# Reordering the last layer's mixing of a three-layer network into one interleaved programme

## The reference

```python
h  = rms(x)*norm1_w*(1+sc1)+sh1          # and hc from the context, the same way
p  = h @ w_in                            # 1024 -> u,v | q | k,v | qh,zf,zb,vh | g
ya = gelu(u) * (w_s @ rms(gelu(v)) + b_s)              # 4 heads of 64
q, k = rope(rms(q)*q_norm_w), rope(rms(k)*k_norm_w)    # 8 query heads, 2 key heads
yb = softmax(q @ [k,kc].T / 8) @ [v,vc]                # 256 queries, 512 keys
# gated recurrence in both directions, 4 heads of 64; log_f, key from zf (forward), zb (backward)
s_new  = exp(b_last)*s + (key*exp(b_last-b)).T @ vh     # state from the context first
o      = (qh*exp(b)) @ s + (scores within a chunk, each with its own decay) @ vh
yc = rms(o_forward + o_backward)*hgrn_norm_w * silu(g)
x  = x + g1 * (concat(ya, yb, yc) @ w_out)
h2 = rms(x)*norm2_w*(1+sc2)+sh2          # then router and 32 experts
```

## Time and profile before

| | |
|---|---|
| median of 3 runs | 1739.26 us (1736.14 to 1740.77) |
| profiled execution | 1736.32 us |
| its span | 1734.5 us |
| PE, DVE, ACT, POOL busy | 93%, 27%, 21%, 2% of the span |
| DMA, mean over the span | 309 GB/s |

### The profile page before, as it was taken

How to read it: one execution, slowest core, us unless ns; L and a number is a source line. 1 busy time by engine, 2 the same in 40 slices (tenths; PEclk the granted TensorE clock), 3 DMA queues, 4 the chain that set the end, 5 groups by cost and what they waited for, 6 DMA issues and landing times.

```text
span 1734.5 us, 20614 instructions
## 1 busy us (share of the span) xinstructions
PE 1617.4 (93%) x8418; PEld 901.9 (52%) x8418; DVE 473.0 (27%) x1118; ACT 368.1 (21%) x770; POOL 34.0 (2%) x44
## 2 busy tenths in 40 slices
PE   5999879999989988999998996897799999999998
PEld 3664654444465647444444782345644444444444
DVE  2044331212123234312122123463311212121212
ACT  2142221111122234211112311442211111111111
POOL 0000000000000000000000001040000000000000
PEclk9999989999999998999999996897799999999999
DMA  9996649999999567699998100004269999999995
GB/s 320 386 386 246 245 166 427 428 429 428 414 335 331 194 243 321 281 427 428 428 429 329 49 1 0 1 1 194 97 286 425 429 429 429 429 429 428 428 427 238
DMA packets 94672, 535.17 MB, mean 309 GB/s; under 512 B 7935, under 2 KB 11737, under 8 KB 69922
## 3 DMA queue, kind: packets, MB, share of 16 engines
q1 hardware_dynamic: 94258, 534.41, 75.8%
q10 hardware_dynamic: 368, 0.12, 0.0%
HBM read 533.44 MB, written 1.06 MB: 308 GB/s over the span
## 4 chain that ended last, share of the span: by engine, by line
PE 85%; DMA 5%; DVE 4%; SPq 2%; ACT 2%; issue 1%; DVEq 0%; POOL 0%; ACTq 0%
PE pair L901 24%; PE bank L890 7%; PE pair L908 6%; PE bank L630 6%; PE bank L908 6%; DMA ring<-in_w_dram 4%; PE bank L637 3%; PE bank L591 3%; PE bank L951 3%; PE pair L951 3%; PE bank L724 2%; SPq L403 1%; DMA ring<-in_a_w_qkv_dram 1%; PE bank L1047 1%; PE pair L1112 1%
## 5 line engine op out<-in xcount | busy, mean ns | idle before, releaser
L901 PE MATMUL pair<-ring,arena 128*64 128x512 f32 x2048 | 447.3, 594 | 3.5 <-DVE arena L1837 2.9
L901 PEld LDWEIGHTS pair<-ring,arena 128*64 128x64 f32 x2048 | 144.7, 137 | 288.1 <-issue 288.1
L890 PE MATMUL bank<-arena 128*128 128x128 f32 x1120 | 139.5, 279 | 9.4 <-DVE arena L1825 9.4
L1850 DVE TENSOR_TENSOR arena<-sq,pair 128x512 f32<-128x512 f32 x32 | 34.0, 1061 | 408.2 <-PE pair L901 408.2
L890 PEld LDWEIGHTS bank<-arena 128*128 128x128 f32 x1120 | 133.6, 196 | 9.9 <-issue 9.9
L630 PE MATMUL bank<-hh,ring 128*128 128x256 f32 x512 | 120.6, 394 | 6.9 <-ACT hh L1206 3.5
L908 PE MATMUL pair<-ring,arena 128*64 128x512 f32 x512 | 116.9, 598 | 0.0
L908 PE MATMUL bank<-ring,arena 128*64 128x512 f32 x512 | 115.3, 592 | 0.0
L630 PEld LDWEIGHTS bank<-hh,ring 128*128 128x128 f32 x512 | 99.4, 197 | 28.0 <-issue 11.6
L1376 ACT ACTIVATE sq<-pair 128x512 f32<-128x512 f32 x32 | 19.1, 597 | 370.3 <-PE pair L901 370.3
L1858 DVE COPY arena<-bank 128x512 f32<-128x512 f32 x32 | 22.1, 692 | 202.7 <-PE bank L908 202.7
(11 more groups left out here) (375 smaller groups left out, 1623.3 us busy)
## 6 DMA issues: line engine op xcount, KB each, us to landing
ring<-in_w_dram SPq DMA_DIRECT2D x96, 2048.0 KB, 15.6
ring<-in_moe_w_gate_dram SPq DMA_DIRECT2D x32, 2048.0 KB, 11.6
ring<-in_moe_w_up_dram SPq DMA_DIRECT2D x32, 2048.0 KB, 15.9
ring<-in_moe_w_down_dram SPq DMA_DIRECT2D x32, 2048.0 KB, 13.9
ring<-in_ada_w_dram SPq DMA_DIRECT2D x24, 2048.0 KB, 17.4
ring<-in_w_mod_dram SPq DMA_DIRECT2D x12, 2048.0 KB, 12.2
ring<-in_a_w_qkv_dram SPq DMA_DIRECT2D x6, 2048.0 KB, 19.2
ring<-in_b_w_qkv_dram SPq DMA_DIRECT2D x6, 2048.0 KB, 11.7
```

What stands on the lines that cost most here:

```text
L890: last = mm(b[part][:, cols(k % 4)], h_tok[:, t, cols(k)], pick[:, t, :], start=(t == 0), stop=(t == TT - 1))
L901: last = mm(b[2 + m][half(a), :], x_sel[:, k, half(a)], R8[moe_slot(l, a, m)][:, k, :], start=(k == 0), stop=(k == KT - 1))
L1850: tt(hid.rearrange("p (f q) -> p q f", f=FT), by_row(gate_act), by_row(b[3]), ALU.mult).then_inc(M["hid_ready"], 1)
```

## The change

The work of the last layer's mixing is the same; its order and some of its shapes are new.

- The gates' part of the projection is split: the context's 256 columns in four parts (`decay_part`), the first at the end of the second layer's experts and three before the new norm is ready, then the tokens' 256 columns. Then vh, g, qh, k; q, vb, vm and u come later, between steps of the recurrence.
- The recurrence runs both directions in one loop of 16 steps (`steps`, `products`, `decayed`), its state from `update_bank` b[0] to b[3]; each sum over features is two matmuls of half the columns into two neighbouring groups of 32 partitions. State terms accumulate in b[6], opened by a matmul with zeros. `norm_sums`, the spreads, rotations and doublings of q and k stand between steps.
- The heads are done in pairs, 8 units of two heads and 128 queries: one maximum over 2 x 512, negated by the instruction itself, two exponentials, two divisions, eight transposes, two copies; scores and values of the two heads alternate between the halves of the array. The chunk scores, ya and the norm of the recurrence's output stand between units.
- The output projection is in two halves of the 1024 inputs: the first half (`out_first`, two output tiles at a time in b[6]) between the last units, the second after them; both are added to `xT`.
- SP loads the first output chunk after POOL's last addition, the second after the last step, and the first experts' chunks wait for their own slots. `state` now lies in the slot of the second output chunk.

The diff, cut to its core:

```diff
-        IN_ORDER = (3, 4, 0, 1, 2)
+        IN_ORDER = (3, 4, 2, 1, 0)
...
+        add_out(2, 1, 32 + 16)
...
-                            sp.wait_ge(out_ps, 3)
+                            sp.wait_ge(update_ps, 4)
...
+            after_experts(1, moe_at[1], 5)
+            sp.wait_ge(arg_ready, 2 * SUB)
+            load(out_at[2][0])
+            sp.wait_ge(out_ps, 1)
+            load(out_at[2][1])
...
+            def decay_part(idx, at):
+                if idx >= 4:
+                    pe.wait_ge(in_ready, idx - 3)
+                w = chunk_in(in_at)
+                for k in range(KT):
+                    if idx == 4:
+                        pe.wait_ge(h_ready, turn(h_ready))
+                    last = mm(b[idx % 4][:, 0:S], w[:, k, cols(idx % 4)], hh[:, k, at:at + S], start=(k == 0), stop=(k == KT - 1))
+                last.then_inc(in_proj, 1)
...
+                if l == 1:
+                    pe.wait_ge(h_ready, turn(h_ready, KT))
+                    decay_part(0, S)
...
+                def query_in(j):
+                    if j == 0:
+                        pe.wait_ge(act_step, 7)
+                    else:
+                        pe.wait_ge(in_ready, EVAC["k"] + j - 1)
+                    part(17 + j, (x1, x0)[j % 2][:, 0:S], 1, lambda w, k: (w[:, k, cols(j)], hh[:, k, 0:S])).then_inc(in_proj, 1)
...
+                def mix_value_in(t):
+                    pe.wait_ge(norm_ready, 42 if t == 0 else 45)
...
+                def steps(i):
+                    for d in range(2):
+                        q = 2 * i + d
+                        pe.wait_ge(prod_ready, q + 1)
+                        for hp in range(2):
+                            at = 64 * d + 32 * hp
+                            last = mm(seen_part(b[7][at:at + 32, 0:S], q), heads_to(key_of(q)[1]), prod_half(q, hp),
+                                      start=(i == 0), stop=(i == SUB - 1))
+                        last.then_inc(sc_ps, 1)
+                    for d in range(2):
+                        if i >= 1:
+                            pe.wait_ge(state_ready, 2 * i + d)
+                        j = sub_chunk(d, i)
+                        own = slice(j * SUB, (j + 1) * SUB)
+                        for hp in range(2):
+                            for m in range(2):
+                                last = mm(b[6][half(m), hp * S + own.start:hp * S + own.stop], state[half(m), d, hp, i, :],
+                                          qq[half(m), d, hp, own], start=False, stop=False)
+                    if i == SUB - 1:
+                        last.then_inc(out_ps, 1)
...
+                    for m in range(2):
+                        last = mm(score2_pair(u)[:, m, :], q2[half(m), p_, cols(qt)], kd[half(m), p_ // 2, :],
+                                  start=True, stop=True)
...
+                    pe.wait_ge(prob_ready, 16 + u + 1)
+                    if u >= 1:
+                        pe.wait_ge(probT_ready, 16 + u)
+                    for m in range(2):
+                        for kt in range(4):
+                            last = nc.tensor.transpose(b[m][:, cols(kt)], p2[:, u % 2, m, cols(kt)], ident)
...
+                def values(p_):
+                    pe.wait_ge(probT_ready, 16 + 2 * p_ + 2)
+                    if p_ >= 1:
+                        pe.wait_ge(o_ready, 16 + p_ + 1)
+                    for kt in range(4):
+                        for m in range(2):
+                            last = mm(b[7][half(m), 0:S], vb[:, kt, half(p_ // 2)], pT2[:, m, kt, :],
+                                      start=(kt == 0), stop=(kt == 3))
+                    last.then_inc(pv_ps, 1)
...
+                def out_first(n):
+                    if n == 0:
+                        pe.wait_ge(ymix_ready, 2)
+                        pe.wait_ge(o_ready, 19)
+                    else:
+                        pe.wait_ge(x_half, 16 + 2 * n)
+                    w = R4[slot_of_chunk(out_at[2][0])]
+                    chunk_in(out_at[2][0])
+                    for c in (2 * n, 2 * n + 1):
+                        for k in range(4):
+                            last = mm(b[6][:, c % 2 * S:(c % 2 + 1) * S], w[:, k, cols(c)], ymix[:, k, :],
+                                      start=(k == 0), stop=(k == 3))
+                    last.then_inc(out_proj, 2)
...
+                steps(0)
+                query_in(1)
+                steps(1)
+                steps(2)
+                query_in(2)
+                steps(3)
+                steps(4)
+                query_in(3)
+                steps(5)
+                steps(6)
+                value_in(0)
+                steps(7)
...
+                steps(11)
+                rotate_queries(0)
+                steps(12)
+                rotate_queries(1)
+                rotate_keys()
+                mix_value_in(1)
+                steps(13)
...
+                scores(5)
+                out_first(0)
+                transposes(4)
+                scores(6)
+                out_first(1)
+                transposes(5)
+                values(2)
+                scores(7)
+                out_first(2)
+                transposes(6)
+                transposes(7)
+                out_first(3)
+                values(3)
+                for c in range(KT):
...
+                query(0)
+                decayed(0)
+                decayed(1)
+                query(1)
+                decayed(2)
+                decayed(3)
...
+                def products(i):
+                    for d in range(2):
+                        q = 2 * i + d
+                        dve.wait_ge(prod_exp, q + 1)
+                        pr = prod_of(q)
+                        tt(pr, pr, qh.rearrange("p b (j t) -> p (b j) t", t=SUB)[:, :, seen_by(*key_of(q))],
+                           ALU.mult).then_inc(prod_ready, 1)
+                        if i < NSUB - 1:
+                            advance(d, i)
...
                 def maxima(u):
+                    dve.wait_ge(scores_ps, 16 + u + 1)
+                    nc.vector.tensor_reduce(stat[:, u % 4, 0:2], score2_pair(u)[:, :, :], AX.X, ALU.max,
+                                            negate=True).then_inc(max_ready, 1)
...
+                maxima(5)
+                half_out(0)
+                weights(4)
+                maxima(6)
+                half_out(1)
+                weights(5)
+                maxima(7)
+                half_out(2)
+                weights(6)
+                weights(7)
+                half_out(3)
...
```

More of the change, by code:

```diff
@@ new lines, in own_values @@
+                def own_values(hp):
+                    pe.wait_ge(dmT_ready, 2 * hp + 2)
+                    for t in range(TT):
+                        for d in range(2):
+                            for m in range(2):
+                                last = mm(b[6][half(m), hp * S + t * P:hp * S + (t + 1) * P], vh[:, t, half(2 * hp + m)],
+                                          dmT[:, d, 2 * t + m, :], start=False, stop=(hp == 1 and t == TT - 1 and d == 1))
+                    last.then_inc(out_ps, 1)
@@ L1069, in hybrid @@
[L1069 to L1075 removed]
+                for t in range(4):
+                    first_part(8 + t, 4, lambda w, k: (hh[:, k, cols(t)], w[:, k, 0:256]))
+                for j in range(2):
+                    first_part(12 + j, 4, lambda w, k: (w[:, k, cols(2 + j)], hh[:, k, 0:S]))
@@ new lines, in hybrid @@
+                steps(14)
+                double_keys(1)
+                mix_gate_in(0)
+                steps(15)
+                mix_gate_in(1)
+                scores(0)
+                pe.wait_ge(act_step, 8)
+                pe.wait_ge(in_ready, EVAC["u0"])
+                for t in range(TT):
+                    last = nc.tensor.transpose(x0[:, cols(t)], sc_rows[:, cols(t)], ident)
+                last.then_inc(sc_ps, 1)
+                turn_scores(0)
+                turn_scores(1)
@@ new lines, in hybrid @@
+                scores(1)
+                mix()
+                own_values(0)
+                transposes(0)
+                turn_scores(2)
+                turn_scores(3)
+                transposes(1)
+                own_values(1)
+                scores(2)
+                values(0)
+                out_sums()
+                scores(3)
+                transposes(2)
+                out_spread()
+                scores(4)
+                transposes(3)
+                values(1)
+                scores(5)
@@ new lines, in hybrid @@
+                nc.vector.reciprocal(rstd[0:64, :], rt[0:64, :]).then_inc(rs_ready, 1)
+                products(9)
+                products(10)
+                rescale(0)
+                rescale(1)
+                products(11)
+                rescale(2)
+                products(12)
+                rope(0)
+                rope(1)
+                products(13)
+                rope(2)
+                products(14)
+                products(15)
+                maxima(0)
```

(1 more changed line is left out.)

761 lines of the change are left out of this document (398 added, 363 removed).

## The result

The changed kernel takes 1689.47 us (median of four executions, 1686.49 to 1694.90), the kernel before beside it 1739.15. The ratio is 0.972 with a 95% interval of 0.970 to 0.974: 2.8% faster, inside the range, 6.5 us above the forecast. In the first set of experiments it took 1688.06, a ratio of 0.971 (0.969 to 0.973).

The account below looks back on a forecast made before the run. The bound was taken as a dependency chain beside a waiting PE in the last layer's mixing. Stages summed to 243.5 us against 303.7, 60 gained, net 55 after 5 to 6 for the clock: forecast 1683 us, range 1662 to 1705.

Parts of the forecast that it names:

- A: Entry and gates of the last layer's mixing: 29.5 us after the change against 39.3 before, 10 us gained.
- F: Second half of the output projection: 2.16 us a tile, eight times 17.3, and 0.7 at the end, 18 us.
- B: Projections vh, g, qh and k: 34.5 us, with the decays beside them just covered.
- C: From the keys to the first state: 10.5 us, the recurrence starting near 1006 us.
- D: The recurrence with everything between its steps: 77 us, of which PE's work is 67, ending near 1083 us.
- rival 1: Narrow pairs don't run side by side: recurrence 8 us longer, heads 7 longer, 1698 us in all; chance 0.14.
- E: The heads, with the first half of the output projection moved in: 74 us at full clock, to 1157 us.
- 2: Rival: the clock stays at half through the heads, 29 us on the chain less 5 counted, 1707 us; chance 0.09.
- 3: Rival: the recurrence pays the whole round trip, 77 us becomes 156, total time 1762 us; chance 0.03.
- 4: Rival: expert weights are late, PE waits for DMA at the first expert, +10 us, 1693 us; chance 0.02.

## Why the prediction was right, point by point

*A.* 31.1 us against 29.5. The norm's sums were taken at 0.12 us a record; they take 3.45 for sixteen, 0.216 each, the 0.43 for two that the prediction's own F took from the earlier trace rows. The cover by the context parts is as forecast: no idle time, and the experiment that undoes the entry shows 8.5 us.

*B and C.* 34.9 and 11.0 against 34.5 and 10.5. The decays were just covered, with no wait in the stage.

*D.* 74.7 against 77, TensorE busy for 67.4 where 67 was summed. That 67 was met is in part luck: the steps take 18.2 us instead of 23 (sums over features 8.5 for 11, states 9.7 for 12) and what stands between them 49.2 instead of 44, 2.8 of it the half clock at 1020.91, which the prediction held at 1.00. The waits are 7.4 us instead of 10, and they stand where the prediction put them: at the first step, at steps 2, 4, 6 and 8 and at the rotation, and none at 1, 3 and 5. The narrow products run side by side, more so than assumed: four groups at once instead of two, which is rival 1 refuted. How much the work between the steps saves was not priced by itself; undone it costs 10.5 us, in waits and clock together.

*E.* 81.2 against 74 and 5 to 6 for the clock. With the clock held the stage is 73.1: the forecast at full clock stands to 1 us, though its parts less well. There the first output part comes after 39.5 us where 42 was summed, the fourth after 67.1 (66), and the last stretch is 6.0 us instead of 8. The term mis-sized is the clock, 8 us instead of 5 to 6. The milestones as it stands: first transposes 13.3 us after the start (13), first output part 44.4 (42), rounds of 8.6 to 13.2 where 8.05 was taken, since the one with the values is longer. That the output part and its addition lie on the chain was right, and the experiment with the division first shows it. Not seen was the other place of the same kind: the norm's root behind two exponentials, 5.3 us of wait.

*F.* 18.0 against 18, 2.16 us a tile.

*Behind the mixing.* Forecast at no change; norm and router took 1.9 us more. The router's sixteen pairs now run at half rate throughout, where the kernel before had the first five steps from pair to pair at 0.22 to 0.25 us.

Together: 52.8 gained in the mixing instead of 55, then 1.9 and 1.5 lost beside it. (The prediction's 1736.3 - 55 with 2.9 added is 1684.2; it wrote 1683.) Of the 52.8 us, the three parts that were undone one by one stand for 8.5 (entry), 10.5 (work between the steps) and 10.5 (output between the heads) by their stages. The narrow products, both directions in one loop and the pairs of heads were not undone, and their shares rest on the sum and the windows alone. Of the rivals, 2 (half clock all through the heads) was true of 7 or 8 of its 29 us, 3 fell with the first profile (the longest wait of the recurrence is 1.48 us), and for 4 no wait for a DMA stands before the first expert.

## What to carry to other kernels

Where two in-order engines feed each other, look for an instruction that waits at the head of a queue while the one behind it, on which the other engine waits, has its inputs: one such change of order took 9.4 us here without removing any work; a second one beside it took 4 us more from the rest of the stage (55.6 to 51.8), which the time doesn't separate from noise. Price a chained stage twice, at the full and at the half clock, and ask which waits make it fall; filling them with harmless matmuls shows the price at once. Judge an interleaving against the same work in a row at the same clock: here the row showed no more idle time, but TensorE ran at half rate where it would have waited. And before two profiles of a stage are compared, compare a part of it that the edit does not touch.

## What the runs showed that was not expected

- The sums over features of both directions, eight records into four 32-column groups, take 0.55 us from start to start at 240 columns, about what four records take (0.56 at 256).
- The same instructions of the recurrence took 73.1, 74.7, 76.4 or 78.1 us in eleven profiles, 1.6 to 1.7 us apart, at clocks of 0.98, 0.95, 0.93 and 0.91 where these were read. The start of the heads took 13.8 to 14.2 us or 17.6 in the same way.
- Work that only keeps TensorE busy made the kernel faster by 7.4 us (clock held), and the stretch from router to experts by 4.0 us against the same kernel without it.
